# Empty slots of an expert block: an index past the gather's bound in place of row 0

## What is computed

```python
def grouped_experts(xf, e_idx, gate, w_gate, w_up, w_down):
    ...
    # assignments sorted by expert and padded per expert to whole blocks of rows;
    row_tok = jnp.full((P,), N, jnp.int32).at[dest].set(flat_tok[order])
    x_pad = jnp.concatenate([xf, jnp.zeros((1, D), xf.dtype)], axis=0)
    def one_block(args):
        toks, e = args
        xb = x_pad[toks]
        hb = jax.nn.silu(xb @ w_gate[e]) * (xb @ w_up[e])
        return hb @ w_down[e]
    yb = lax.map(one_block, (row_tok.reshape(n_blocks, EXPERT_BLOCK), blk_e))
    yb = yb.reshape(P, D) * row_w[:, None].astype(yb.dtype)
    return jnp.zeros((N + 1, D), yb.dtype).at[row_tok].add(yb)[:N]
```

## Time and profile before

| | us |
|---|---|
| median of 3 runs | 1317.84 |
| lowest, highest | 1317.26, 1319.43 |
| the profiled execution, span | 1317.98 |

### The profile page before, as it was taken

One profiled execution on the slowest core, in us unless ns is written; L12 is line 12 of the kernel. 1 busy time (PEld: TensorE's weight loads), 2 busy tenths in 40 slices (PEclk: granted clock), 3 DMA queues, 4 the chain that ended last, 5 costly groups with the idle time before them and its releaser, 6 DMA issues.

```text
span 1318.0 us, 11746 instructions
## 1 busy us (share of the span) xinstructions
PE 1065.8 (81%) x4504; PEld 557.5 (42%) x4504; DVE 439.3 (33%) x683; ACT 212.1 (16%) x543; POOL 111.5 (8%) x185
## 2 busy tenths in 40 slices
PE   6999999989999999899955777777777777777760
PEld 4776444454445467765542223333322222222220
DVE  4038743576521230132362222222222222222215
ACT  0125432341112011111000111110011110111111
POOL 3000000131321000000000000000000000000005
PEclk9999899989999999999967988888888888888885
DMA  9311300411216311101664999999999999999806
GB/s 294 137 64 65 131 0 1 164 69 68 96 30 218 128 64 64 64 1 23 237 216 164 396 397 397 397 397 397 397 397 396 396 396 396 397 396 396 330 20 215
DMA packets 129332, 290.36 MB, mean 220 GB/s; under 512 B 11536, under 2 KB 13456, under 8 KB 129296
## 3 DMA queue, kind: packets, MB, share of 16 engines
q1 hardware_dynamic: 114176, 267.02, 54.6%
q0 software_dynamic: 3760, 13.63, 2.8%
q10 hardware_dynamic: 11360, 9.22, 2.2%
HBM read 266.52 MB, written 23.33 MB: 220 GB/s over the span
## 4 chain that ended last, share of the span: by engine, by line
PE 78%; DVE 12%; issue 4%; ACT 3%; DMA 2%; POOL 1%; SPq 0%; ACTq 0%; POOLq 0%; DVEq 0%
PE bank L416 22%; PE bank L404 12%; PE bank L737 12%; PE bank L723 9%; PE bank L724 9%; DVE arena L1598 4%; PE bank L420 2%; PE bank L650 2%; PE bank L728 1%; PE score_pair L712 1%; PE score_pair L628 1%; DVE arena L1589 1%; PE bank L543 1%; DVE arena L1602 1%; DVE arena L1600 1%
## 5 line engine op out<-in xcount | busy, mean ns | idle before, releaser
L416 PE MATMUL bank<-arena 128*128 128x512 f32 x640 | 285.6, 603 | 3.6 <-DVE arena L1239 1.1
L723 PE MATMUL bank<-arena 128*64 128x512 f32 x544 | 238.8, 596 | 25.0 <-DVE arena L1589 25.0
L724 PE MATMUL bank<-arena 128*64 128x512 f32 x544 | 238.1, 597 | 0.0
L416 PEld LDWEIGHTS bank<-arena 128*128 128x128 f32 x640 | 121.1, 192 | 154.3 <-issue 148.9
L737 PE MATMUL bank<-arena 128*64 128x512 f32 x544 | 152.1, 722 | 16.4 <-DVE arena L1602 16.4
L404 PE MATMUL bank<-arena 128*128 128x288 f32 x640 | 158.5, 410 | 1.3 <-DVE arena L1239 1.3
L404 PEld LDWEIGHTS bank<-arena 128*128 128x128 f32 x640 | 122.4, 192 | 35.8 <-DVE arena L1239 1.7
L723 PEld LDWEIGHTS bank<-arena 128*64 128x64 f32 x544 | 73.5, 138 | 91.2 <-issue 91.2
L728 PE MATMUL bank<-arena 128*128 128x128 f32 x68 | 19.0, 434 | 112.2 <-DVE arena L1600 112.2
L1595 DVE TENSOR_TENSOR arena<-bank,arena 64x512 f32<-64x512 f32 x34 | 23.4, 689 | 251.5 <-ACT arena L1200 251.5
L1023 ACT ACTIVATE arena<-bank 128x512 f32<-128x512 f32 (+5 forms) x125 | 56.5, 489 | 313.3 <-PE bank L404 113.1
(11 more groups left out here) (239 smaller groups left out, 952.7 us busy)
## 6 DMA issues: line engine op xcount, KB each, us to landing
arena<-in_exp_w_gate_dram SPq DMA_DIRECT2D x33, 2048.0 KB, 13.4
arena<-in_exp_w_up_dram SPq DMA_DIRECT2D x33, 2048.0 KB, 17.0
arena<-in_exp_w_down_dram SPq DMA_DIRECT2D x33, 2048.0 KB, 15.8
arena<-in_w_in_dram SPq DMA_DIRECT2D x7, 2048.0 KB, 8.4
expert_rows<-arena ACTq DMA_DIRECT2D x68, 128.0 KB, 5.5
expert_rows<-arena SPq DMA_DIRECT2D x1, 4608.0 KB, 14.2
out_dram<-arena SPq DMA_DIRECT2D x4, 1024.0 KB, 10.5
arena<-in_w_mem_k_dram SPq DMA_DIRECT2D x2, 2048.0 KB, 9.5
```

The source lines that it names most:

```text
L416: ins = mm(b[:, :], x, w[:, k, :], start=k == 0, stop=k == KC - 1)
L723: mm(g, x, wexp[j][0][:, k, :], start=k == 0, stop=k == KC - 1)
L724: ins = mm(u, x, wexp[j][1][:, k, :], start=k == 0, stop=k == KC - 1)
```

## The change

Token numbers are shifted by -4096 before they are summed into slots, and 4096 is added to the sum; so a filled slot gets its token's number, as before, and an empty slot gets 4096. The gather gets a bound, the last row of `hn_rows`, and an index past it is not an error. Since rows of `xg` may then be left unwritten, VectorE fills the whole tile with zeros once, ahead of the routing.

```diff
+NOROW = 4096
...
                 g.indirect_dma_start(out=xg, out_offset=None, in_=hn_dram,
-                                     in_offset=bass.IndirectOffsetOnAxis(ap=gidx, axis=0)).then_inc(xg_ld, 16)
+                                     in_offset=bass.IndirectOffsetOnAxis(ap=gidx, axis=0),
+                                     bounds_check=TOK - 1, oob_is_err=False).then_inc(xg_ld, 16)
...
             ve.wait_ge(pool_c, 2)
-            n.step(v.tensor_copy(tokf, tok_i))
+            n.step(ts(tokf, tok_i, -float(NOROW), None, ALU.add))
...
             ve.wait_ge(v_free, V.drained)
+            n.step(v.memset(xg, 0.0))
             n.settle()
             glog = lg[:, :, 0:GROUPS]
...
             b = V.take(ve)
-            V.done(v.tensor_copy(sidx, b[:, 0:NB // 2]))
+            V.done(ts(sidx, b[:, 0:NB // 2], float(NOROW), None, ALU.add))
```

## The result

| | median, us | lowest to highest | executions |
|---|---|---|---|
| before | 1318.22 | 1316.3 to 1319.43 | 8 |
| changed | 1322.18 | 1320.43 to 1324.6 | 8 |

The ratio is 1.0028, 95% interval 1.002 to 1.0037: slower by 3.7 us, 2.6 to 4.9. The forecast was 1318.4 with a range from 1315.6 to 1321.4, so this set lies above the range.

What follows compares the result with a forecast made beforehand. PE, with VectorE's and ScalarE's steps between its products, was taken to bound the loop, not the transfers. Memset +0.91, first gather -0.3 and the rest 0 gave +0.6 us on 1317.84: 1318.4 us, range 1315.6 to 1321.4.

Steps and rivals of the forecast that it cites:

- What bounds the loop: Expert loop: PE with VectorE's and ScalarE's steps sets the pace; no PE wait is on weight loads, so fewer transfers bring 0.
- The sum at the loop's start: Delay up to the first expert pair: 0.91 - 0.3 + 0 = +0.6 us, ends -0.25 and +2.2.
- memset: VectorE's new fill of the gather's tile before the router's first reduction: +0.91 us, all on the path, ends 0.85 and 0.96.
- the bound on GpSimd: GpSimd's issue of the first gather with a bound: 0 us, ends -0.3 and +1.26.
- the first gather's landing: First gather's issue to PE's first transpose, 37 of 128 rows empty: -0.3 us, ends -0.8 and 0.
- What the loop makes of it: Over the pairs a start shift shrinks; one execution's end moves about 0 or 3.5 us, but over executions +0.6 stands.
- rival of the missed return: First gate products start late enough to miss the clock's return: 1317.84 + 3.5 = 1321.3 us, 12 in 100.
- The choice to let the sum stand over executions: Whole kernel: clock steps need not fall alike each time against the program's start, so +0.6 us was kept over executions.

Runs made afterwards that it cites:

- e6: The changed kernel with seven products that nobody reads in PE's idle time of each pair, ahead of the transposes; 1306.25 us, ratio 0.9912.
- e5: The kernel before with seven products that nobody reads in PE's idle time of each pair, ahead of the transposes; 1312.44 us, ratio 0.9952.
- e8: The kernel before with two memsets of the gather's tile in a row, at the place of the changed kernel's one; 1321.20 us, ratio 1.002.
- e11: The kernel before with no edit, run for a second trace; 1325.93 us.
- e12: The kernel before with no edit, run for a third trace; 1320.46 us.
- e14: The kernel before measured against itself, no edit; ratio 0.9994.
- e3: The kernel before with only the bound given to the gather, all indices inside it, so all rows still fetched; ratio 0.9995.
- e1: The changed kernel with the memset moved to VectorE's idle time behind the last one-hot; 1320.46 us, ratio 1.0009.
- e2: The kernel before with only the memset of the gather's tile added; 1321.10 us, ratio 1.002.
- e4: The kernel before with four memsets of the gather's tile in a row, ahead of the routing; 1324.72 us, ratio 1.0042.

## Why the prediction was wrong

**What bounds the loop** was right: PE's waits are unchanged, the transfers' relief shows in the landing times and is worth nothing. The Trainium skill (Perfetto Trace Analysis, "Identifying the Most-Contended Engine") would have had the transfers optimised first. In the kernel before this gained nothing; once PE's pairs were quicker than the 34.35 us that the transfers take, the same cut gained 6.2 us (e6 against e5). At its 34.13 us a pair the kernel before was a little ahead of the transfers already, as the prediction says, and only its lead, 24 us against landings of 12.5 to 15.6, kept it from waiting.

**The sum at the loop's start is the step that failed**: +0.6 forecast, +1.39 measured in the first pair of traces and 1.5 over all of them.

| term | forecast | measured |
|---|---|---|
| memset | +0.91 | 0.91, and 0.28 of idle time ahead of it: +1.19 |
| the bound on GpSimd | 0, ends -0.3 and +1.26 | +0.47 |
| the first gather's landing | -0.3, ends -0.8 and 0 | -0.27, over more traces about -0.1 |

The memset's own duration, from two rows of other widths, was met to the nanosecond (911 and 912). The idle time ahead of it was put at nothing, though the row that gave the price shows 0.2 us of it; in e8 the second of two memsets begins 0.28 us behind the first, too. The bound's 0 was the choice of the nearest row; the cost isn't in the instruction (1.31 us against 1.26) but ahead of it. The gather's -0.3 was a choice between two ends that nothing in the trace could decide, and its closeness to 0.27 is luck. By the Trainium skill's fixed partitions for each DMA engine (DMA: Bandwidth & Descriptors, "The descriptor swizzle") the gain would be 0; a gain of some 0.1, less than the scatter, does not decide against that.

A right sum would have given 1317.84 + 1.5 = 1319.3 us, inside the range, and the three sets of the changed kernel have medians of 1322.18, 1321.42 and 1319.91. So the sum is not all of the miss. The first set is the highest of the three, and 1322.18 holds some chance.

**"What the loop makes of it"** was right in kind. The prediction saw that pairs settle on 34.13 whatever the start, and that a start that misses the clock's return costs about 3.5 us in one execution; the traces show steps of 3.41 and the end 612.0 us behind the return. Its rival of the missed return, given 12 in 100, is what the first two traces show: in the kernel before the first products began 34.26 us after the fall, in the changed kernel 35.37, and among the twelve traces the decision lies between 34.26 and 35.01. Settled pairs take 34.13 in the changed kernel as well, so nothing in the loop makes up for it. Its first pair lasted to 737.21, 37.74 us, against 36.02 before.

```profile
737.21 1.09 PE L713 MATMUL score_pair<-arena 128*128 128x128 f32 x8
```

But the missed return is no property of the change: e11, e12 and e14, traces of the kernel before, missed it as well. That the first trace of before is the one of four that did not is luck of the execution. What the change can do is make the miss more frequent; the counts of quick executions speak for that, but by how much is not measured directly.

The choice to let the sum stand over executions is therefore not refuted. The mean moved by +2.1 us with a standard error of 0.37; 1.39 lies two of these below, 1.5 a little less, and a whole step of 3.41 more than three above. The means of the other sets, each against its runs of the kernel before, point the same way: +0.2 (e3), +1.1 (e1), +2.1 (e2), +2.6 (e8) and +5.6 us (e4), with standard errors of 0.4 to 1.0, for delays of 0.36, 0.53, 1.05, 2.35 and 4.61 us. Whether the excess of 0.6 or 0.7 over the delay is chance, and why the fall and the start keep the distances that they do from execution to execution, stays open.

One reading was off: the prediction sets the profiled span, 1317.98 us, beside the median of the device times, 0.14 above it. Wherever a run has both, the device time is 1.7 to 1.9 us above the span, so that execution took some 1319.7 us, more than the median of its kernel, in spite of its early return; its fall came at 668.38, in e12 and e14 at 665.70 and 665.60. And the range's lower end, 1315.6, is worked out from the median of before (1317.84 - 0.25 - 2), not from the forecast.

## What to carry to other kernels

Full transfer engines bound nothing while no engine waits for a load; look at the waits and at whether landing times grow. Once the pace of the compute engine comes within a per cent of the transfers', saving bytes is worth nothing alone and much together with the step that quickens the compute (here -6.2 us on top of e5's -5.9). And where the clock of PE falls ahead of a long loop, a small delay can cost one execution nothing or a whole step of the clock's return (3.41 us here); over many executions its own length is the fair price as far as these runs can tell (2.1 us, standard error 0.37, for 1.5). One trace of either kernel does not tell this: take several, and price the idle time ahead of a new instruction as well as its duration. Better, keep PE at work so that the clock doesn't fall.

## What the hardware showed that was not expected

- A row skipped by the bound still is a packet: 3760 in the software queue with and without the 1024 rows, 4.19 MB less. The gather's whole transfer got shorter all the same: a settled pair's lands after 6.9 us in a late stretch, 7.7 before, though early in the loop, at 735 to 769 us, after 8.6 in both.
- A bounded indirect transfer costs 0.48 us more ahead of its first issue, 0.20 ahead of the second (0.53 against 0.33), and 0.05 in the instruction.
- From the clock's return in the first pair of the loop, at 705.6 to 712.2 us, to the end twelve executions of seven kernels took 611.7 to 612.3 us, whatever came before.
